# The sample's first norm and first projection block placed ahead of the last quarter of the prompt's candidate search

## What is computed

```
h  = rmsnorm(x, norm1_w) * (1 + sc1) + sh1
u  = h @ w_in                              # 1024 x 2584: SSD, DeltaNet, Fourier, attention columns
y  = concat(ssd(u), gdn(u), fnet(u), attention(u)) @ w_out
x  = x + g1 * y
h2 = rmsnorm(x, norm2_w) * (1 + sc2) + sh2
x  = x + g2 * peer(h2)

peer: q = h2 @ w_q; s = q . sub_keys                      # 8 heads, 2 halves, 128 keys each
      top 16 of each half -> sums of pairs -> top 16       # the candidate search
      act = gelu(u_tab[idx] . h2);  out = (softmax(best) * act) @ v_tab[idx]
```

## Time and profile before

| | |
|---|---|
| median of three runs | 2671.66 us |
| span of the profiled execution | 2676.8 us |
| PE busy | 1763.4 us (66%) |
| DVE busy | 1612.3 us (60%) |
| POOL busy | 1458.7 us (54%) |
| ACT busy | 365.9 us (14%) |

### The profile page before, as it was taken

One profiled execution on the slowest core, in us unless ns is written; L12 is line 12 of the kernel. 1 busy time (PEld: TensorE's weight loads), 2 busy tenths in 40 slices (PEclk: granted clock), 3 DMA queues, 4 the chain that ended last, 5 costly groups with the idle time before them and its releaser, 6 DMA issues. The chain is left out here.

```text
span 2676.8 us, 28082 instructions
## 1 busy us (share of the span) xinstructions
PE 1763.4 (66%) x10274; PEld 1079.0 (40%) x10274; DVE 1612.3 (60%) x4086; ACT 365.9 (14%) x905; POOL 1458.7 (54%) x1540
## 2 busy tenths in 40 slices
PE   6978588778984111079889797878993000078888
PEld 5857577646634111044244286755551000011111
DVE  2425898871589998941108288982399999910000
ACT  3222221112112000010111131112110000000000
POOL 0000454443666676767765544433566777777776
PEclk8999698978996555589999898878996555599999
DMA  9488697666999999999999987766999999999999
GB/s 392 155 337 329 249 405 263 217 240 223 404 409 421 420 420 420 420 364 414 406 419 420 380 334 300 246 212 251 350 406 384 420 420 420 420 419 420 413 419 373
DMA packets 249496, 959.36 MB, mean 358 GB/s; under 512 B 32400, under 2 KB 33680, under 8 KB 231568
## 3 DMA queue, kind: packets, MB, share of 16 engines
q0 software_dynamic: 221184, 805.40, 75.8%
q1 hardware_dynamic: 19584, 142.62, 13.3%
q10 hardware_dynamic: 8592, 9.56, 1.0%
HBM read 955.11 MB, written 2.36 MB: 358 GB/s over the span
## 5 line engine op out<-in xcount | busy, mean ns | idle before, releaser
L559 POOL DMA_INDIRECT sb_ring<-in_peer_u,sb_idxu x768 | 728.5, 949 | 745.5 <-DVE sb_idxT L1985 288.6
L559 POOL DMA_INDIRECT sb_ring<-in_peer_v,sb_idxT x768 | 730.0, 951 | 458.7 <-issue 213.7
L2017 DVE CUSTOM_DVE_ANT_0 sb_ring<-sb_ring,pv 128x1024 f32<-128x1024 f32 x768 | 905.9, 1217 | 30.4 <-DMA sb_ring<-in_peer_u,sb_idxu 24.6
L582 PE MATMUL pv<-sb_ring,sb_wcol 128*32 128x512 f32 x3072 | 649.7, 616 | 72.0 <-DMA sb_ring<-in_peer_v,sb_idxT 62.7
L582 PE MATMUL pb<-sb_hT,sb_wring 128*128 128x256 f32 (+1 forms) x1920 | 378.6, 358 | 49.9 <-ACT sb_big L1120 27.3
L582 PEld LDWEIGHTS pb<-sb_hT,sb_wring 128*128 128x128 f32 x1920 | 324.4, 205 | 124.3 <-issue 71.5
L582 PEld LDWEIGHTS pv<-sb_ring,sb_wcol 128*32 128x32 f32 x3072 | 125.2, 110 | 542.1 <-DMA sb_ring<-in_peer_v,sb_idxT 367.9
L585 PE MATMUL pb<-sb_cst,sb_dots 128*128 128x128 f32 x6 | 2.4, 401 | 406.8 <-DVE sb_dots L2023 406.8
L582 PE MATMUL pb<-sb_big 128*128 128x128 f32 (+2 forms) x1888 | 228.3, 283 | 19.3 <-DVE sb_big L1699 12.7
L582 PEld LDWEIGHTS pb<-sb_big 128*128 128x128 f32 (+1 forms) x1888 | 220.1, 196 | 37.5 <-DVE sb_big L1699 16.1
L2054 DVE TENSOR_TENSOR sb_big<-pv,sb_big 128x512 f32<-128x512 f32 x4 | 2.7, 686 | 317.7 <-PE pv L582 317.7
(11 more groups left out here) (239 smaller groups left out, 1629.0 us busy)
## 6 DMA issues: line engine op xcount, KB each, us to landing
sb_ring<-in_w_mod_blocks SPq DMA_DIRECT2D x38, 1024.0 KB, 7.6
sb_wring<-in_w_in_blocks SPq DMA_DIRECT2D x34, 1024.0 KB, 7.7
sb_wring<-in_w_q_blocks SPq DMA_DIRECT2D x26, 1024.0 KB, 8.5
sb_wring<-in_w_out_blocks SPq DMA_DIRECT2D x14, 1024.0 KB, 7.7
sb_ring<-in_peer_u,sb_idxu POOLq DMA_INDIRECT x768, 9.3
sb_ring<-in_peer_v,sb_idxT POOLq DMA_INDIRECT x768, 7.7
sb_wring<-in_w_mod_blocks SPq DMA_DIRECT2D x10, 1024.0 KB, 8.0
sb_ring<-in_w_in_blocks SPq DMA_DIRECT2D x6, 1024.0 KB, 15.2
```

What stands on the lines that cost most here:

```text
L559: pool.indirect_dma_start(ring[:, j, :], None, a["tab_" + kind][l_of(q)], bass.IndirectOffsetOnAxis(ap=of, axis=0)).then_inc(rows_in[j], 16)
L582: return nc.tensor.matmul(out, lhsT, rhs, start=start, stop=stop)
L2017: dve.tensor_tensor_reduce(out=row, in0=row, in1=pv[:, :, :].rearrange("p a b -> p (a b)"), scale=1.0, scalar=0.0, op0=ALU.mult, op1=ALU.a ...
```

## The change

The sample's norm0 stage keeps its place in the list but now stands ahead of the last eight modulation steps (the table gives them to topk of unit 0 and not to the end of query). The DVE's half of norm1 of unit 1 is done inside the prompt's search, ahead of its fourth quarter, and waits there for the copy of h2 on ACT. PE's `st_topk(0, 0)`, the transpose of the indices, moves behind the block tok 0 of unit 1, ahead of `sums`. ACT's `st_topk(0, 0)` and the two exponentials of softplus move behind the copies of channel block 5. The DVE's `st_topk(0, 0)` keeps its place behind the search.

```diff
 FIRST_WEAVE = {
-    "att0": ({0: 1, 1: 1, 2: 1}, 1), "out": ({3: 4}, 0), "query": ({0: 4}, 8), "topk0": ({}, 0)}
+    "att0": ({0: 1, 1: 1, 2: 1}, 1), "out": ({3: 4}, 0), "query": ({0: 4}, 0), "topk0": ({0: 8}, 0)}
@@ schedule
             if (st, u) == ("topk0", 0):
-                main.append(("mix", "norm0", 1))
+                main += [("mix", "norm0", 1), ("firstquads",)]
+                continue
@@ PE, st_proj, behind the tok blocks
                         release_block(b, "tokcols_full", (u, k, nt - 1))
+                        if k == 0 and u == 1:
+                            st_topk(0, 0)
                         if k == 0:
                             sums(u)
@@ PE and ACT, st_topk
-                gap(u, f"topk{i}", 0)
+                if u:
+                    gap(u, f"topk{i}", 0)
@@ ACT, st_proj
-                fn(sca[:, 8, 0, 0:16], pr("A"), ACT.Exp)
-                act.wait_ge(*done("neg_abs", u))
-                fn(sca[:, 2, 0:nt, :], sca[:, 1, 0:nt, :], ACT.Exp).then_inc(*tick("exp_neg", u))
+                def exponents():
+                    fn(sca[:, 8, 0, 0:16], pr("A"), ACT.Exp)
+                    act.wait_ge(*done("neg_abs", u))
+                    fn(sca[:, 2, 0:nt, :], sca[:, 1, 0:nt, :], ACT.Exp).then_inc(*tick("exp_neg", u))
+
+                if u != 1:
+                    exponents()
...
                         fn(cin[:, k % 2, 2:2 + NC], pb[:, k % 2, 0:NC]).then_inc(*tick("proj_copied", (u, k)))
+                        if u == 1 and point == 1:
+                            st_topk(0, 0)
+                            exponents()
@@ DVE, norm
+                if u == 1 and not which:
+                    dve.wait_ge(*done("h2_copied", (0, 0, 1)))
                 dve.wait_ge(*done("rms_read", (u, which)))
...
-                if not which and u < 2:
+                if not which and u == 0:
                     gap(u, "norm1", 0)
@@ DVE, st_query
                 for k in range(4):
+                    if u == 0 and k == 3:
+                        norm(1, 0)
                     gap(u, "query", 4 * k + 4)
@@ DVE, stages and items
-            stages = {"norm1": lambda u: norm(u, 0), "proj": st_proj,
+            stages = {"norm1": lambda u: gap(1, "norm1", 0) if u == 1 else norm(u, 0), "proj": st_proj,
...
-                                        "end": item_end, "gaterow": item_gaterow, "last": item_last}, stages)
+                                        "end": item_end, "gaterow": item_gaterow, "last": item_last,
+                                        "firstquads": lambda: st_topk(0, 0)}, stages)
```

More of the change, by code:

```diff
@@ L1111, in _ @@
                                         "v": item_v, "end": item_end, "gaterow": item_gaterow, "xrows": item_xrows,
-                                        "outrows": item_outrows}, stages)
+                                        "outrows": item_outrows, "firstquads": lambda: gap(0, "topk0", 0)}, stages)
             run()
@@ L1505, in _ @@
                                         "gaterow": item_gaterow, "xrows": item_xrows, "outrows": item_outrows, "last": item_last,
-                                        "final": item_final}, stages)
+                                        "final": item_final, "firstquads": lambda: gap(0, "topk0", 0)}, stages)
             run()
```

## The result

The changed kernel takes 2686.78 us (median of 14 runs, 2672.47 to 2696.03), beside 2672.51 us for the kernel before (14 runs, 2668.2 to 2691.38, the three of the forecast among them). The ratio is 1.0047, with a 95% interval of 1.0029 to 1.0064: slower, as forecast, but the time lies 6.8 us above the forecast and 2.3 us above the upper end of the range. The medians differ by 14.3 us and the means by 12.3 ± 2.3 us. Two later comparisons of the same pair gave 1.0030 (1.0014 to 1.0045) and 1.0042 (1.0026 to 1.0059).

The account below looks back on a forecast made before the run. DVE was taken to bound the kernel on both sides of the seam (search to sample's projection); softplus delay and clock loss gave +7.7 to +9.4 us, taken as +8.3: 2671.7 + 8.3 = 2680.0 us, range 2670.0 to 2684.5.

Parts of the forecast that it names:

- What bounds the kernel: Prompt's search and sample's projection behind it (the seam): DVE sets the pace; PE's lead can gain at most 10.2 us.
- The new wait: Behind the search, at the cast of the transposed indices: DVE stands still 13.2 us until PE's transpose behind tok 0 ends.
- What goes out of the way to softplus: DVE from cast to softplus: 21.05 us lose the norm (3.99) and waits for gathered rows (4.8), leaving nearer 12.0.
- Where PE's lead goes: PE ahead of `sums`: stops 24 us in place of 0.7, loses its 16.4 us lead and stands 7.8 us behind.
- The term for the clock: PE's block behind the stop at `sums`: up to 1.2 us more lost if PE starts at the low clock.
- A: PE's projection blocks at full clock: tok 0 ends at 299.1, time 2675.7, no measurable change; chance 0.19 together with B.
- B: DVE's 4.4 us of waits for convolution inputs vanish: +3.9 us, 2675.6; chance 0.19 together with A.
- C: Not slower: transpose ends before 302.5, at full clock 299.6; at best 2.9 us shorter, 2668.8; chance 0.07.
- D: PE leaves its stop at low clock, two more waits of some 2 us in the projection: +12.5 us, 2684.2; chance 0.11.
- the base of the sum: Whole kernel's time before the change, taken as the median 2671.66 us, to which +8.3 us was added.
- The range: Whole kernel's time: 2670.0, down to C's side of A and B, up to D, 2684.5.

Follow-up runs that it names:

- e4_twice: Against the changed kernel: matmuls of tok 0 of unit 1 done twice, ahead of the transpose; ratio 1.0056, +15.3 ± 1.7 us over the kernel before.
- e0_after: The changed kernel again, no edit, beside the kernel before on the same chip; median 2687.25 us, ratio 1.0030.
- e3_norm: Against the changed kernel: transpose of indices and exponential of gates back ahead of the whole projection, early norm kept; ratio 1.0021, +4.9 ± 1.6 us over the kernel before.
- b2_before: The kernel before, unedited, run in the place of a changed one; median 2679.12 us, ratio 1.0007.
- e5_mod: The kernel before with only the table edit that moves the eight modulation steps; median 2674.44 us, ratio 0.9995.
- e5b_mod: The kernel before with only the table edit of the modulation steps, a second time on another chip; median 2678.49 us, ratio 0.9992.

## Why the forecast was right and where it was wrong

**What bounds the kernel** was right: DVE on both sides of the seam. It waits for 8.5 and 10.6 of some 161 us in the two profiles of the kernel before, and `e4_twice` shows that a wait put into its list comes out at the end of the seam: 7.3 us of wait, 6.9 us of seam.

**The new wait** was right: 13.2 us forecast, 12.5, 11.4 and 12.5 measured, by the same instruction and released by PE's transpose. The error of 0.7 us comes from conv 4 and 5, which ran in 9.70 in place of 10.02 us, and from the transpose, which took 0.27 in place of 0.48 us. In `e0_after` conv 4 and 5 took 8.59 us, and the wait is shorter by the same 1.1 us.

**What goes out of the way to softplus**, the norm (3.99) and the waits for rows (4.8), was right: from the cast to softplus are 11.4 us in the trace of after, 12.0 forecast. That the norm ahead of the search's end costs something by itself was in the reckoning only as a later gather; `e3_norm` puts it at +3.8 us of seam, and it is hidden under the longer wait.

**Where PE's lead goes** was right, with 24 us of stop forecast and 23.99, 24.25 and 23.97 measured. The term for the clock, up to +1.2 us, was too small. The first profiles alone nearly hide it: conv 6 and 7 behind the stop took 8.57 us, against 8.84 in the earlier trace rows. The second ones, `b2_before` and then `e0_after`, do not:

```profile
321.37 1.48 PE L582 MATMUL pb<-sb_lat,sb_cst 128*128 128x8 f32 x12 [1.65 <-ACT sb_zs L1120]
322.70 7.15 PE L582 MATMUL pb<-sb_hT,sb_wring 128*128 128x256 f32 x32
```

```profile
330.26 2.71 PE L583 MATMUL pb<-sb_lat,sb_cst 128*128 128x8 f32 x12 [24.25 <-ACT sb_zs L1124]
332.81 9.56 PE L583 MATMUL pb<-sb_hT,sb_wring 128*128 128x256 f32 x32
```

`sums` took 2.71 us at a granted clock of 0.50 (1.2 GHz) in all three profiles of the changed kernel, behind a stop of 24 us, and 1.48 us at 1.00 (2.4 GHz) in both of the kernel before, behind a wait of 0.7 to 1.7 us. From its start to the end of the block behind it are 11.4 us on average, against 9.3. With it DVE waits 1.8 us more for convolution inputs, which the forecast had only shift; that the one comes from the other is likely, and no run takes them apart.

**That the sum came out at 8.3 is in part luck.** Softplus starts 6.5 us later on average, where 7.7 to 8.2 were forecast, mostly because the wait is 12.1 and not 13.2 us. Behind softplus the seam loses 1.7 us more, where 0 to 1.2 were forecast. Two errors of over 1 us have offset each other, in averages of two and three profiles.

**The rivals.** A (PE's block fast) did not come: the row of the 24 columns above has a granted clock of 0.50 through a block in which PE is busy for 6.82 of 6.82 us, as in the earlier trace rows. By the rule of the Trainium skill (TensorE: Matmul & The Clock Gate, Part 1: The HAM clock gate), that sustained activity releases the throttled clock, part of this block ought to have run fast; the rows disagree with it a second time. B (4.4 us absorbed) did not come, the waits for convolution inputs are 4.9 us. C (not slower) would have needed a transpose that ends before 302.5, and it ended at 303.85, in an execution that came to the search 1.0 us sooner. D (two more waits of some 2 us) did not come as told: PE did leave its stop at the low clock, but the seam is +8.3 us and not +12.5.

**The step that failed is the base of the sum.** The part on how the numbers follow says "The median is 2671.66 us. Forecast: 2671.7 + 8.3 = 2680.0". The +8.3 us is what the seam measured, and the difference of the times is 9.8 ± 1.0; but the kernel before is by its 131 runs a kernel of 2678 us, and 2678.0 + 8.3 is 2686.3, where 2686.78, 2687.25 and 2688.85 were measured. Of the 7.7 us between the forecast and the 2687.7 of all runs of the changed kernel, 6.3 are the base and some 1.5 the difference. Three runs of a kernel whose runs scatter by 5.8 us had come out together at the low end.

This rests on the later runs. In the first comparison by itself the base was off by only 0.9 us (2672.51 against 2671.66), and nearly the whole miss stood in the difference, 14.3 us by the medians in place of 8.3. Its 12.3 ± 2.3 us by the means and the 8.3 are less than two standard errors apart, and the later comparisons gave 9.6 and 10.2.

A sign of it lay open: each run's time in this study is about 1.8 us above its own span, so the profiled execution before, with a span of 2676.8, had a time of about 2678.6 (an estimate), above all three runs shown, and I noted the 5.1 us between span and median and then added to the median. The sum on the span's own time would have given 2678.6 + 8.3 = 2686.9. That it fits so well is luck too, for it is a single execution: the one profiled of `b2_before`, at 2673.16 us, would have given 2681.5.

**The range** failed by the same step. It was built from the rivals alone, and had no term for the scatter of the kernel before; some 3 us for the error of three runs (5.8 us over the root of 3, known from the later runs only), toward the side on which the span lay, would have held the time.

What stays open: whether the kernel before was faster in the first comparison or only drawn low, and whether the 1.5 us between the seam's +8.3 and the time's +9.8 ± 1.0 is anything. Outside of the seam the averages of the profiles differ by 0.7 us, and the errors cover the rest.

## What to carry to other kernels

Before an engine that waits is given work from further down, look at what that work is put in front of: a transpose of 0.3 us on PE held the engine that bounds the stage for 12 us, because 23 us of lead work stood ahead of it, and the work gained nothing since the bounding engine's own list had not become shorter. Move an instruction of the bounding engine only if what it then delays does not start a chain of its own, as the end of the search starts the gathers. And before adding a reckoned difference to a time, compare the span of the profile with the runs: when it lies above all of them by several us, the few runs may be a low draw, and the base and the range must say so.

## What the runs showed of the hardware

I had not expected one and the same kernel to run in visibly different ways. The stretch of unit 3 from PE's first attention matmul (`sb_qkv`, `sb_big`) to the first matmul of the output projection takes 19.7 us in six of the fourteen profiles, with the clock granted in full, and 24.3 us in seven, with a mean granted clock of 0.73 or 0.74 (and 25.5 us at 0.67 in the first of the kernel before). The columns are those of the earlier trace rows. The first row is from `e5_mod`, the second from `e5b_mod`, the same kernel:

```profile
1824.15:1843.85 19.70, 14.49 (x118) 10.03 (x117) 5.47 (x10) 7.18 (x21) 10.31 (x11) 1.00 0.96 366
```

```profile
1829.09:1853.35 24.26, 19.20 (x119) 14.60 (x117) 5.46 (x10) 7.62 (x21) 10.93 (x12) 0.74 0.86 330
```

And so for the changed kernel, in its first profile and in `e0_after`:

```profile
1833.67:1857.94 24.27, 19.20 (x119) 14.60 (x117) 5.47 (x10) 7.62 (x21) 10.94 (x12) 0.74 0.86 327
```

```profile
1832.27:1851.97 19.70, 14.48 (x118) 10.02 (x117) 5.47 (x10) 7.18 (x21) 10.31 (x11) 1.00 0.95 353
```

In `e5b_mod` the granted clock is 1.00 up to 1839.59 us and 0.50 from 1841.09 on. PE was busy for 0.29 us of the 1.5 us ahead of that and for 0.81 us of the 1.5 us in which the clock fell; in `e5_mod` it was busy for 0.28 and 0.81 us at the same place, and the clock stayed at 1.00. What decides between the two these profiles do not show.

Both durations come up with the transpose moved and without it, so the 4.6 us are no effect of the change; a single profile against a single profile would have shown them as one. Over the whole program it is the same: in the 35 runs of the kernel before that stood beside `e0_after`, the mean granted clock of a run lies between 0.824 and 0.833 and goes with its time (correlation -0.83), at 1.9 us for each 0.001. So the scatter of 5.8 us goes with the clock; that the clock makes the time, and not the reverse, is seen in the stretch above only, where the same 14.5 us of PE's matmuls at a full clock become 19.2 us.
